# Six projection slots of a mixer as three float32r products of split parts, in a ring of six weight slots

## The reference, cut to what matters

```python
proj = jnp.einsum('btd,de->bte', x, w_in)
(a_q, a_k, a_v, a_decay, a_beta, a_gate, c_glu, f_q, f_k, f_v, f_forget) = split_columns(proj, IN_SIZES)
qkv = jax.nn.silu(causal_depthwise_conv(jnp.concatenate([a_q, a_k, a_v], -1), gdn_conv_w))
a_q, a_k, a_v = jnp.split(qkv, 3, axis=-1)
log_decay = -jnp.exp(gdn_a_log) * jax.nn.softplus(a_decay + gdn_dt_bias)
o_a = gated_delta_rule(heads(a_q), heads(a_k), heads(a_v), log_decay, beta)
u = glu_a * jax.nn.sigmoid(glu_b)
u = causal_depthwise_conv(u, cnv_dw_w) + cnv_dw_b
```

## Time and profile before

| | us |
|---|---|
| median of 3 runs | 2197.59 |
| lowest and highest | 2194.07, 2197.79 |
| span of the profiled execution | 2199.7 |
| the first mixer's slots 0 to 7, on TensorE | 8.3 to 74.8 |
| the second mixer's slots 0 to 7, on TensorE | 390.9 to 453.0 |

### The profile page before, as it was taken

One profiled execution on the slowest core, in us unless ns is written; L12 is line 12 of the kernel. 1 busy time (PEld: TensorE's weight loads), 2 busy tenths in 40 slices (PEclk: granted clock), 3 DMA queues, 4 the chain that ended last, 5 costly groups with the idle time before them and its releaser, 6 DMA issues.

```text
span 2199.7 us, 31791 instructions
## 1 busy us (share of the span) xinstructions
PE 2150.1 (98%) x12075; PEld 1799.4 (82%) x12075; DVE 1594.4 (72%) x1644; ACT 1217.3 (55%) x1204; POOL 159.8 (7%) x232
## 2 busy tenths in 40 slices
PE   8999999999999999999999999999999999999998
PEld 7987888898778888888888888888788887877886
DVE  3676554576788988989898988989866429866453
ACT  4254443415467777777776777777664323655442
POOL 1200000310300000000000000000066010000000
PEclk9999999999899999999999999999999999999999
DMA  9134555422599999999999999999846554535552
GB/s 346 56 111 154 183 190 186 140 74 83 187 332 351 352 371 352 361 349 359 348 358 351 362 370 349 364 350 361 298 154 195 191 147 148 170 101 160 189 191 77
DMA packets 240787, 537.25 MB, mean 244 GB/s; under 512 B 18006, under 2 KB 120448, under 8 KB 240320
## 3 DMA queue, kind: packets, MB, share of 16 engines
q1 hardware_dynamic: 236560, 521.11, 67.0%
q0 software_dynamic: 3168, 9.07, 1.6%
q10 hardware_dynamic: 976, 5.91, 0.6%
HBM read 534.71 MB, written 1.31 MB: 244 GB/s over the span
## 4 chain that ended last, share of the span: by engine, by line
PE 87%; DVE 7%; issue 2%; ACT 2%; DMA 1%; DVEq 0%; SPq 0%; ACTq 0%
PE bank L1311 9%; PE bank L1313 9%; PE bank L1312 9%; PE bank L1452 8%; PE bank L1448 8%; PE bank L1449 8%; PE bank L1037 6%; PE bank L1475 4%; PE bank L1476 4%; PE bank L1480 4%; PE bank L1612 2%; PE bank L1035 2%; DVE weights_lo L2408 2%; PE bank L1420 1%; PE bank L1594 1%
## 5 line engine op out<-in xcount | busy, mean ns | idle before, releaser
L2408 DVE TENSOR_TENSOR weights_lo<-ring_data,weights_hi 128x2048 fp32r<-128x2048 f32 x336 | 760.3, 2290 | 93.4 <-ACT weights_hi L2089 91.8
L2089 ACT ACTIVATE weights_hi<-ring_data 128x2048 fp32r<-128x2048 f32 x336 | 637.9, 1919 | 171.9 <-DMA ring_data<-in_moe_w 170.9
L1448 PE MATMUL bank<-weights_hi,xg_hi 128*128 128x512 f32 x896 | 352.3, 393 | 2.6 <-DVE arena L2866 2.6
L1449 PE MATMUL bank<-weights_hi,xg_lo 128*128 128x512 f32 x896 | 349.5, 390 | 0.0
L2403 DVE TENSOR_TENSOR weights_lo<-ring_data,weights_hi 128x2048 fp32r<-128x2048 f32 x98 | 227.5, 2352 | 49.5 <-ACT weights_hi L1864 49.5
L1452 PE MATMUL bank<-weights_lo,xg_hi 128*128 128x512 f32 x896 | 240.5, 390 | 0.1
L1312 PE MATMUL bank<-weights_lo,xT_hi 128*128 128x512 f32 x584 | 229.2, 393 | 0.0
L1311 PE MATMUL bank<-weights_hi,xT_hi 128*128 128x512 f32 x520 | 206.4, 397 | 1.7 <-issue 0.7
L1313 PE MATMUL bank<-weights_hi,xT_lo 128*128 128x512 f32 x520 | 203.3, 391 | 0.0
L1448 PEld LDWEIGHTS bank<-weights_hi,xg_hi 128*128 128x128 f32 x896 | 168.5, 188 | 37.1 <-issue 3.0
L1452 PEld LDWEIGHTS bank<-weights_lo,xg_hi 128*128 128x128 f32 x896 | 168.7, 188 | 35.8 <-DVE weights_lo L2408 0.5
(11 more groups left out here) (514 smaller groups left out, 3227.8 us busy)
## 6 DMA issues: line engine op xcount, KB each, us to landing
ring_data<-in_moe_w SPq DMA_DIRECT2D x672, 512.0 KB, 4.4
ring_data<-in_ffn_w_in SPq DMA_DIRECT2D x88, 512.0 KB, 4.7
ring_data<-in_w_in SPq DMA_DIRECT2D x70, 512.0 KB, 4.6
ring_data<-in_ffn_w SPq DMA_DIRECT2D x66, 512.0 KB, 4.1
ring_data<-in_ffn_w_out SPq DMA_DIRECT2D x44, 512.0 KB, 4.0
ring_data<-in_w_out SPq DMA_DIRECT2D x24, 512.0 KB, 4.7
ring_data<-in_w_in SPq DMA_DIRECT2D x8, 396.0 KB, 4.1
ring_data<-in_w_in SPq DMA_DIRECT2D x8, 390.0 KB, 5.5
```

Source lines behind the costliest of these rows:

```text
L1448: mm(o, xg_hi[:, k, :], e_hi(at)[:, r], start=k == 0, stop=False)
L1449: mm(o, xg_lo[:, k, :], e_hi(at)[:, r], start=False, stop=False)
L2089: nc.scalar.activation(e_hi(at), ring_data[:, e_slot(at), :], ACT.Copy).then_inc(ring.hi_done, 1)
L2408: v.tensor_tensor(e_lo(at), ring_data[:, e_slot(at), :], e_hi(at), ALU.subtract).then_inc(ring.lo_done, 1)
```

## The change

Slots 2 to 7 of both mixers are multiplied as three float32r products. ScalarE splits the tokens into a high part (`mx_hi`) and VectorE into a low part (`mx_lo`), both in the arena; ScalarE makes each slot's high part and puts it into the ring slot three places further on, VectorE leaves the low part in the slot itself. So a slot's high part takes the place of the load three further on, and SyncE's queue now has loads 5 to 10 wait until project(m - 3) has been counted. TensorE waits for the high part instead of the load, and for the low part ahead of the third product; it makes the two products with the high part first. ScalarE's splits stand between its copies: slot 2 after the softplus, slots 3, 4 and 5 ahead of the copies of slots 1, 2 and 3, slot 6 after that of slot 3, slot 7 after that of slot 4. VectorE's low parts stand ahead of its first tile (slots 2 and 3), of tiles 2, 4 and 6 (slots 4, 5 and 6) and after the last tile (slot 7); that of the tokens stands ahead of its gates.

Beside that, the memory's rows (`memx`) are loaded into `lnp`, since the arena's place is taken, and POOL loads the first layer norm's parameters there after its part of the first mixer, once the memory's squares are taken. Two semaphores of their own (`exp_a`, `npass_ready`) become steps of shared ones.

```diff
+MIX_SPLIT = range(2, 8)
+MIX_XLO_AT = 18944
-        memx = arena[:, at_fs:at_fs + TT * D].rearrange("p (j d) -> p j d", j=TT)
+        memx = lnp
+        mx_hi, mx_lo = (split_parts(f"mx_{k}", "arena", o, DT, T) for k, o in (("hi", 0), ("lo", MIX_XLO_AT)))
+        def mix_parts(l, m):
+            n, w = (MIX_LOADS + FFN_LOADS) * l + m, 8 * PROJ[m][1]
+            return (lo_slots[:, (n + k) % RING, 0:w].rearrange("p (k c) -> p k c", k=DT) for k in (RING // 2, 0))
 # SyncE, mixer: ahead of ring.load(sp, n0 + m, ...)
+                    if m - RING // 2 in MIX_SPLIT:
+                        sp.wait_ge(ring.used, n0 + m - RING // 2 + 1)
 # POOL
                 if u:
                     pool.wait_ge(sem("ln_done"), LN_DONE[u])
+                else:
+                    pool.wait_ge(sem("act_stage"), stage("mem_sq1"))
             for l in range(DEPTH):
-                layer_norm_params(2 * l)
                 if l == 0:
                     memory_weights(0)
+                else:
+                    layer_norm_params(2)
                 mixer(l)
+                if l == 0:
+                    layer_norm_params(0)
 # TensorE, project(m, g)
+                        if m in MIX_SPLIT:
+                            pe.wait_ge(sem("mix_hi"), mix_split(l, m))
+                        else:
+                            ring.arrived(pe, n0 + m)
+                    if m in MIX_SPLIT:
+                        o, c = bk(b, 2, T)[:, g], slice(P * g, P * g + P)
+                        w_hi, w_lo = mix_parts(l, m)
+                        if (m, g) == (MIX_SPLIT[0], 0):
+                            pe.wait_ge(sem("mix_lo"), mix_split(l, None))
+                        for k in range(DT):
+                            mm(o, w_hi[:, k, c], mx_hi[:, k, :], start=k == 0, stop=False)
+                            mm(o, w_hi[:, k, c], mx_lo[:, k, :], start=False, stop=False)
+                        if g == 0:
+                            pe.wait_ge(sem("mix_lo"), mix_split(l, m))
+                        for k in range(DT):
+                            i = mm(o, w_lo[:, k, c], mx_hi[:, k, :], start=False, stop=k == DT - 1)
+                        if g == 1 or w == P:
+                            i.then_inc(ring.used, 1)
+                        return
 # ScalarE, mixer
+                def mix_high(m):
+                    n = n0 + m
+                    ring.arrived(act, n)
+                    if n >= RING // 2:
+                        act.wait_ge(ring.used, n - RING // 2 + 1)
+                    a_(next(mix_parts(l, m)), ring.slot(n)[:, 0:8 * PROJ[m][1]].rearrange("p (k c) -> p k c", k=DT), ACT.Copy, "mix_hi")
+                a_(mx_hi[:, :, :], actT[:, :, :], ACT.Copy, "mix_hi")
                 project(0)
                 softplus(0, 0)
+                mix_high(2)
                 for m in range(1, 4):
+                    mix_high(m + 2)
                     project(m)
+                mix_high(6)
                 a_(beta[:, :, :], tokA[:, :, 6:12], ACT.Sigmoid, "act_gate")
...
                     if m == 2:
                         project(4)
+                        mix_high(7)
 # VectorE, mixer: ahead of the gates
+                dve.wait_ge(sem("mix_hi"), mix_split(l, None))
+                v.tensor_tensor(mx_lo[:, :, :], actT[:, :, :], mx_hi[:, :, :], ALU.subtract).then_inc(sem("mix_lo"), 1)
+                def low_part(m):
+                    hi, lo = mix_parts(l, m)
+                    dve.wait_ge(sem("mix_hi"), mix_split(l, m))
+                    v.tensor_tensor(lo, ring.slot(n0 + m)[:, 0:8 * PROJ[m][1]].rearrange("p (k c) -> p k c", k=DT), hi, ALU.subtract).then_inc(sem("mix_lo"), 1)
...
+                low_part(2)
+                low_part(3)
                 for t in range(9):
+                    if t in (2, 4, 6):
+                        low_part(3 + t // 2)
...
+                low_part(7)
                 dve.wait_ge(sem("gdn_act"), 7 * l + 6)
```

More of the change, by code:

```diff
@@ L137 @@
 ONCE = (
-    ("mem_factor", "router_max", "sel_ready", "norm_rows2", "pcol_ready", "lambda_inverse", "row_factor_m", "mk_sumsq", "mk_normed", "blocks_out", "states_ready", "keys_chosen", "heads_sumsq", "heads_normed", "u_split"),
+    ("mem_factor", "router_max", "sel_ready", "norm_rows2", "npass_ready", "pcol_ready", "lambda_inverse", "row_factor_m", "mk_sumsq", "mk_normed", "blocks_out", "states_ready", "keys_chosen", "heads_sumsq", "heads_normed", "u_split"),
     ("norm_rows1", "dt_spread", "angle_reduced", "blocks_ready", "powers_ready", "queries_zeroed"),
-    ("mem_scaled", "mem_sq0", "mem_sq1", "mem_std", "dt_ready", "toep_act", "unit_act", "mk_std", "row_spread", "mkT_act", "heads_std", "gelu_done", "ys_ready"),
+    ("exp_a", "mem_scaled", "mem_sq0", "mem_sq1", "mem_std", "dt_ready", "toep_act", "unit_act", "mk_std", "row_spread", "mkT_act", "heads_std", "gelu_done", "ys_ready"),
     ("router_psum", "place_psum", "y_half", "pcol_psum", "toep_psum", "row_psum", "bc_psum", "mkT_psum", "y_psum", "glu_half"),
@@ L473, in two_block_kernel, with mix_split @@
         xg_hi, xg_lo = (split_parts(f"xg_{k}", "actT", D * i, DT, CAP) for i, k in enumerate(("hi", "lo")))
+        mx_hi, mx_lo = (split_parts(f"mx_{k}", "arena", o, DT, T) for k, o in (("hi", 0), ("lo", MIX_XLO_AT)))
+        def mix_parts(l, m):
+            n, w = (MIX_LOADS + FFN_LOADS) * l + m, 8 * PROJ[m][1]
+            return (lo_slots[:, (n + k) % RING, 0:w].rearrange("p (k c) -> p k c", k=DT) for k in (RING // 2, 0))
+        def mix_split(l, m):
+            return (1 + len(MIX_SPLIT)) * l + (1 if m is None else MIX_SPLIT.index(m) + 2)
         out_hi = [split_parts(f"out_hi{m}", "arena", o, 4, 512) for m, o in enumerate(OUT_HI_AT)]
@@ L729, in _ @@
                 expert_slot("up", 0, m, 0, m, 0)
-            sp.wait_ge(sem("npass_ready"), 1)
+            sp.wait_ge(sem("dve_stage"), stage("npass_ready"))
             npass = sp.value_load(npass_i[0:1, 0:1], min_val=1, max_val=2)
@@ L1024, in project @@
                     if g == 0:
-                        ring.arrived(pe, n0 + m)
+                        if m in MIX_SPLIT:
+                            pe.wait_ge(sem("mix_hi"), mix_split(l, m))
+                        else:
+                            ring.arrived(pe, n0 + m)
                         if m - 2 == GLUA_LOAD:
@@ L1536, in moe @@
                     up_slot(0, m, m, FFN_LOADS + m + 1)
-                pe.wait_ge(sem("npass_ready"), 1)
+                pe.wait_ge(sem("dve_stage"), stage("npass_ready"))
                 last = pe.value_load(npass_i[0:1, 1:2], min_val=E - 1, max_val=2 * E - 1)
@@ L1952, in softplus @@
                     a_(lg1[:, :, c], lg1[:, :, c], ACT.Ln, "act_gate", bias=1.0)
+                def mix_high(m):
[4 more added lines that the diff above has]
+                    a_(next(mix_parts(l, m)), ring.slot(n)[:, 0:8 * PROJ[m][1]].rearrange("p (k c) -> p k c", k=DT), ACT.Copy, "mix_hi")
+                if l == 0:
+                    act.wait_ge(sem("xT_loaded"), 16)
+                else:
+                    act.wait_ge(sem("xT_dve"), 2 * plain(3))
+                    act.wait_ge(sem("xT_act"), 2 * plain(3))
+                a_(mx_hi[:, :, :], actT[:, :, :], ACT.Copy, "mix_hi")
                 project(0)
@@ L1956, in mixer @@
                     act.wait_ge(sem("params_loaded"), 16)
-                    a_(hpar[:, :, 18:24], hpar[:, :, 12:18], ACT.Exp, "exp_a")
+                    a_(hpar[:, :, 18:24], hpar[:, :, 12:18], ACT.Exp, "act_stage")
                 softplus(0, 0)
+                mix_high(2)
                 for m in range(1, 4):
+                    mix_high(m + 2)
                     project(m)
+                mix_high(6)
                 a_(beta[:, :, :], tokA[:, :, 6:12], ACT.Sigmoid, "act_gate")
@@ L2094, in moe @@
                     a_(ex[:, j], lgt[:, j], ACT.Exp, "router_exp", bias=m1[:, j:j + 1])
-                act.wait_ge(sem("npass_ready"), 1)
+                act.wait_ge(sem("dve_stage"), stage("npass_ready"))
                 last = act.value_load(npass_i[0:1, 1:2], min_val=E - 1, max_val=2 * E - 1)
@@ L2514, in mixer @@
                     st.do(v.memset(uraw[:, :, 0:TAPS - 1], 0.0))
-                    dve.wait_ge(sem("exp_a"), 1)
+                    dve.wait_ge(sem("act_stage"), stage("exp_a"))
                     st.do(v.tensor_scalar(hpar[:, :, 12:18], hpar[:, :, 18:24], -1.0, None, ALU.mult))
@@ L2822, in moe @@
                 st.settle()
-                v.tensor_copy(npass_i[:, :], cnt[:, 1:3]).then_inc(sem("npass_ready"), 1)
-                dve.wait_ge(sem("npass_ready"), 1)
+                v.tensor_copy(npass_i[:, :], cnt[:, 1:3]).then_inc(sem("dve_stage"), 1)
+                dve.wait_ge(sem("dve_stage"), stage("npass_ready"))
                 last = dve.value_load(npass_i[0:1, 1:2], min_val=E - 1, max_val=2 * E - 1)
```

## The result

| | before | after |
|---|---|---|
| median, us | 2195.83 | 2224.52 |
| span of the profiled execution, us | 2199.7 | 2222.8 |

The changed kernel is slower: ratio 1.0127, 95% interval 1.0114 to 1.0140, which is 28.7 us. The forecast had the direction and less than half of the size: 12.6 us, and a range that ended at 2219.

The account below looks back on a forecast made before the run. The prediction took TensorE to bound the kernel, with ScalarE directly behind ahead of the squares. Mixer terms 2.4 and 4.1 us plus clock terms 2.5 and 3.6 summed to 12.6 us slower: median 2210, range 2198 to 2219.

Parts of the forecast that it names:

- The price of a matmul: TensorE, slots 2 to 7: 0.117 us per 256-column float32r matmul, ends 0.107 and 0.120; saves 7.1 us a mixer.
- the weight load: TensorE's split slots: taken as hidden; the rival that it does not hide gave 0.224 us a matmul, 2240, chance 0.04.
- The split of slot 6 rules the squares: ScalarE: this split begins 4.9 us after project(3), so L1067 starts 6.7 us later in the first mixer, 5.0 in the second.
- the last four have the whole inversion to land in: SyncE's queue: each mixer's last four ring loads, queued behind the new waits, land during the inversion and cost nothing.
- the rest of the trace unchanged but shifted: Sign of a right forecast: beyond the named stands, half clock and slot 7 ending 6 us later, nothing else changes.
- The rest at nothing: Later loading of the first layer norm's parameters, moved memory rows and renamed semaphores cost nothing; 4.9 us if cover were gone.
- the first mixer's start: First mixer up to slot 3: project(3) ends at 36.2 us, against 37.2 before.
- the clock: L1067 and the head of slot 6 at half clock after TensorE's stands: +2.5 us in the first mixer, +3.6 in the second.
- The long half clock: Rival: slots 6, 7 and the products between them stay at 1.2 GHz, some 8 us more a mixer; 2226, chance 0.05.
- The faster case: Rival: splits fit ScalarE's idle time and TensorE's saving reaches the end, 14 us; 2183, or 2190 for half; chance 0.12.

Follow-up runs that it names:

- Run 3: The changed kernel with ScalarE's splits of slots 6 and 7 moved behind the last squares and behind slot 5's eviction; ratio to before 1.0065.
- run 5: The changed kernel with unread products added on TensorE ahead of the squares, 72 in the first mixer and 44 in the second; ratio to before 1.0087.
- run 2: The changed kernel with loads 10 to 13 of each mixer held until the inversion's next to last level is applied; ratio to before 1.0076.
- run 4: The kernel before with only the memory's rows moved into `lnp` and the first layer norm's parameters loaded after POOL's first mixer; ratio 1.0016.
- run 6: The changed kernel with only slots 2 to 5 split, at the change's places, and slots 6 and 7 plain; ratio to before 1.0008.
- run 7: The changed kernel with loads 10 to 13 held and the splits of slots 6 and 7 moved behind the squares; ratio to before 1.0027.
- run 10: Only slots 2, 3, 6 and 7 split, at better places with loads and parameters held, slot 7's low part behind the keys' scaling; ratio to before 0.9966.
- run 1: The kernel before with only the changed kernel's waits on SyncE's queue for loads 5 to 10, nothing split; ratio 1.0040.
- run 9: Only slots 2, 3, 6 and 7 split, at better places with loads and parameters held, slot 7's low part ahead of the keys' scaling; ratio to before 0.9987.
- run 8: The changed kernel, all six slots split, with splits and low parts of slots 2, 6 and 7 at new places, loads and parameters held; ratio to before 0.9996.

## Why the prediction was right in direction and wrong in size

**Right.** The price of a matmul, 0.120, lies at the upper end of the terms; the weight load is hidden (24 loads in the 2.88 us of a group). That goes against the rule of the Trainium skill that the prediction weighed (TensorE: Matmul & The Clock Gate, "The mechanism"), though the same section also lets a load into the background weight buffer run ahead of matmuls in flight. The split of slot 6 rules the squares: ScalarE waits 4.1 us for its transfer in both mixers, TensorE stands 5.8 and 9.1 us where 6.4 and 9.6 were forecast, L1105 runs at half clock for 5.28 us where 5.2 was forecast. Run 3 takes the split away from there and gives 13 us back; run 5 fills the idle time alone, and of its 8 us 5.1 lie behind the squares. In the second mixer, up to L1067, the forecast is off by 0.7 us, in part by luck: slot 3 ended 1.0 us later than forecast, and the way from there to L1067 was 0.3 shorter.

**Wrong, the largest step:** "Queued on SP behind such a wait are only later loads; the last four have the whole inversion to land in, so I count nothing for them." They land in time, but their landing is what costs: 3.9 and 5.9 us in the two inversions, by run 2 10.8 us in all. With it fell the sign that the prediction named, "the rest of the trace unchanged but shifted". I asked whether the loads would be late and not what they would meet. The rows to ask it from were there: TensorE's inversion is the densest stretch of instructions in the mixer, and before's own first mixer stood 0.80 us in it with "issue" as releaser.

**Wrong, the same step a second time:** "The rest at nothing" for the layer norm's parameters. Their cover (time until the layer norm) was right, but alone they cost 4.4 us by the medians (0.7 to 6.6 by the interval), of which run 4's trace shows 1.5 in the stretch where they land. Within the changed kernel the two share the stretch, so this is not added to the 10.8.

**Mis-sized: the first mixer's start.** Slot 3 was to end 1.0 us earlier and ended 2.1 later. The prediction had VectorE meet POOL in the second mixer only. In the first, slot 2's low part met POOL's masks and took 4.19 us instead of 2.29, and POOL's mask beside it 2.90 instead of about 0.85:

```profile
23.82 4.19 DVE L2585 TENSOR_TENSOR weights_lo<-ring_data,weights_lo 128x2048 fp32r<-128x2048 f32 x1 [1.42 <-ACT weights_lo L1869]
...
25.81 2.90 POOL L819 TENSOR_TENSOR arena<-consts_sb,small 128x384 f32<-128x384 f32 x1
```

The rows read like waiting in turn: POOL's two masks ahead of this one, at 24.22 and 25.01, took their usual 0.85 and 0.84 us, the low part ended 2.2 us after the second of them, and the mask shown ended 0.70 us after the low part. TensorE stood 2.05 us for it and then ran the eight products of that group in 1.75 instead of 1.12, at half clock, which lasted into the next group. The same stand is in runs 2, 3, 5, 6 and 7 (2.06 to 2.10 us), but of these only run 3 has half clock behind it in the first mixer, so this part of the delay does not follow from the stand alone. In the changed kernel all of it is passed on to ScalarE's split of slot 6, and so to L1067 (+2.9 against the forecast).

**Mis-sized: the clock.** The terms had L1067 and the head of slot 6. Half clock also held L1115 (1.56 instead of 0.93), and the products of slot 2 after the stands of some 2 us there. From L1067 to the end of slot 7 this cost 2.6 us more than forecast in the two mixers together.

**The rivals.** The long half clock came close to the time with the wrong mechanism: slot 7 ran at full pace (5.8 us). The faster case was tied to "slots landing or splits running far quicker"; it needed neither, but other places, as run 10 shows with four slots.

## What to carry to other kernels

A transfer that is moved later is not free because it has time to land: ask which stretch it lands in, and whether an engine there runs many short instructions whose own loading it will hold up. On an engine that takes its work in order, put a new step directly ahead of its use, and behind everything on which the busiest engine waits: moving two splits was worth 13 us here, their duration 3.8 us a mixer. And price the clock with the stand: the changed kernel's stands of 6 and 9 us ahead of the squares cost 4.6 and 5.3 us more behind them. Its stands of 2 us ahead of slot 2 cost some 1.5 us more, but the same stand in the first mixer of runs 2, 5, 6 and 7 cost nothing more.

## What the runs showed of the hardware

**Instruction loading can be held up by other DMA traffic.** The inversion of the second mixer took 21.4 us in eight of the twelve kernels told of here; in the four with the bunched ring transfers in it 25.6 to 27.2, with stands that ended some 2 to 3 us after a packet of the instruction queue. That the missing instructions were TensorE's is read from the queue's packets and from the stands that no other engine released; no row names the engine that a packet is for. Other traffic is not needed for a short stand: before's of 0.80 us came with a DMA share of 0.01, and it too ended 2.0 to 2.5 us after such a packet.

**The half clock does not need a stand.** It followed each of the five stands of 4.9 to 9.4 us ahead of the squares here, whose 24 passes then took 5.28 us each time; behind the two of 2.1 us they took 3.96 and 3.79, and without a stand 2.7 to 3.1. It also came in the second mixer behind the squares, without any stand, in runs 1, 4, 7 and 9 (0.57, 0.62, 0.56 and 0.50 for some 4 us; slot 7 ended 1.5 to 2 us later for it), and not in before or in runs 3, 6, 8 and 10, whose products around it are the same or nearly so. In run 5 it came in both mixers behind a TensorE that had been kept busy. What decides that is open.

**VectorE and POOL hold each other up** when both work on SBUF operands: 4.19 instead of 2.29 us, and 2.90 instead of 0.85. In the second mixer of the changed kernel it is the same: the low part of the tokens took 3.38 us instead of 2.23 and ended 2.15 us after POOL's operation.
